# Hybrid decoder step on one core: output products of a batch moved between the sums of keys and of values, and the first batch of each layer prepared sooner

## What is computed

```python
kvc = _compress(concat([gather(pool_cmp), kv_c]), pe, w1, w2)      # chunk keys and values
# hid = silu(first half of chunk @ w1[:, :16] + second half @ w1[:, 16:]);  kvc = hid @ w2
blocks = _sel_blocks(concat([gather(pool_sel), kv_s]))             # pages by page_table
o_cmp, o_sel = _nsa_global(q_a, pos, kvc, blocks, slopes_a)        # chunk scores pick 16 blocks of 64 keys
o_win = _window_sample(q_a, win_all, n_win, slopes_a)              # last 512 keys
o_dil = _dilated_sample(q_b, dil_all, n_dil, slopes_b)             # strides 1, 4 and 16
y = _merge(o_cmp, o_sel, o_win, gate, o_dil, w_out)                # w_out for all rows together
```

## Time and profile before

| what | us |
|---|---|
| median of 3 runs | 2276.86 (2276.32 to 2280.13) |
| the profiled execution | 2278.07 |
| its span | 2276.2 |
| TensorE busy | 2142.7 (94%) |
| VectorE busy | 913.7 (40%) |
| POOL busy | 730.5 (32%) |
| ScalarE busy | 571.8 (25%) |
| batches of layer 0 | about 353 to 634 |
| batches of layer 1 | about 1471 to 1750 |

### The profile page before, as it was taken

How to read it: one execution, slowest core, us unless ns; L and a number is a source line. 1 busy time by engine, 2 the same in 40 slices (tenths; PEclk the granted TensorE clock), 3 DMA queues, 4 the chain that set the end, 5 groups by cost and what they waited for, 6 DMA issues and landing times.

```text
span 2276.2 us, 42319 instructions
## 1 busy us (share of the span) xinstructions
PE 2142.7 (94%) x12904; PEld 1516.7 (67%) x12904; DVE 913.7 (40%) x2434; ACT 571.8 (25%) x1404; POOL 730.5 (32%) x767
## 2 busy tenths in 40 slices
PE   7999997899899999999999999889989999999998
PEld 4545565676677777777745455657666677777776
DVE  2002763544553222336510147544455523233474
ACT  2101661212213322120111036421221232121202
POOL 0101772122243334434201037612224334343440
PEclk9999998999999999999999999999999999999999
DMA  9642026899964444554375320389999444444441
GB/s 349 235 166 84 19 57 195 279 282 290 287 221 167 172 172 181 195 196 172 119 277 203 131 72 0 91 266 276 293 295 301 172 166 179 173 172 172 180 165 42
DMA packets 130749, 424.92 MB, mean 187 GB/s; under 512 B 18337, under 2 KB 90274, under 8 KB 114082
## 3 DMA queue, kind: packets, MB, share of 16 engines
q1 hardware_dynamic: 108928, 326.01, 40.8%
q10 hardware_dynamic: 21666, 97.06, 14.2%
HBM read 412.40 MB, written 152.57 MB: 248 GB/s over the span
## 4 chain that ended last, share of the span: by engine, by line
PE 82%; DVE 6%; issue 4%; DMA 2%; SPq 2%; ACT 2%; POOL 1%; DVEq 0%; POOLq 0%; ACTq 0%
PE bank L1141 40%; PE bank L1224 14%; PE bank L1435 3%; PE bank L1443 3%; PE bank L1630 2%; PE bank L1404 2%; PE bank L1372 2%; PE bank L1384 2%; DVE zone L2113 2%; PE bank L1237 1%; PE bank L1455 1%; PE bank L1654 1%; POOL zone L975 1%; PE bank L1581 1%; DMA zone<-in_batch_rows 1%
## 5 line engine op out<-in xcount | busy, mean ns | idle before, releaser
L1141 PE MATMUL bank<-zone,ring 128*128 128x288 f32 x1664 | 424.8, 407 | 11.2 <-DVE zone L1793 8.5
L1141 PEld LDWEIGHTS bank<-zone,ring 128*128 128x128 f32 x1664 | 314.8, 190 | 104.2 <-DVE zone L1793 14.0
L1141 PE MATMUL bank<-zone,w 128*128 128x288 f32 x1408 | 353.5, 406 | 0.0
L1224 PE MATMUL bank<-ring,hT 128*128 128x512 f32 (+2 forms) x800 | 329.3, 565 | 6.5 <-ACTq L792 4.9
L1141 PEld LDWEIGHTS bank<-zone,w 128*128 128x128 f32 x1408 | 267.5, 190 | 73.9
L925 POOL TENSOR_TENSOR w<-ring 128x512 f32<-128x512 f32 x72 | 95.0, 1319 | 544.7 <-PE bank L1141 309.8
L1224 PEld LDWEIGHTS bank<-ring,hT 128*128 128x128 f32 (+1 forms) x800 | 147.2, 189 | 157.7 <-issue 151.8
L645 ACT COPY zone<-bank 128x288 f32<-128x288 f32 x72 | 28.7, 399 | 561.9 <-PE bank L1141 561.9
L1141 PE MATMUL bank<-xT,ring 128*128 128x288 f32 x512 | 137.3, 412 | 1.1 <-ACT zone L645 1.1
L1141 PEld LDWEIGHTS bank<-xT,ring 128*128 128x128 f32 x512 | 98.4, 193 | 29.5 <-ACT zone L645 2.0
L956 POOL COPY zone<-zone 128x128 f32<-128x128 f32 (+1 forms) x24 | 9.6, 399 | 327.8 <-ACT zone L710 327.8
(11 more groups left out here) (262 smaller groups left out, 3034.7 us busy)
## 6 DMA issues: line engine op xcount, KB each, us to landing
out_dil_s<-in_state_kv_dil SPq DMA_DIRECT2D x48, 2720.0 KB, 12.1
ring<-in_w_units SPq DMA_DIRECT2D x72, 1024.0 KB, 4.8
ring<-in_cache_kv_cmp SPq DMA_DIRECT2D x256, 128.0 KB, 4.9
ring<-in_cache_kv_sel SPq DMA_DIRECT2D x256, 128.0 KB, 9.0
zone<-in_batch_rows ACTq DMA_DIRECT2D x14, 2112.0 KB
zone<-in_batch_rows ACTq DMA_DIRECT2D x30, 768.0 KB, 6.6
ring<-in_w_in SPq DMA_DIRECT2D x10, 2048.0 KB, 8.0
zone<-in_batch_rows ACTq DMA_DIRECT2D x14, 1088.0 KB, 5.2
```

The source lines that it names most:

```text
L1141: last = mm(dst[:, 0:HALF], lhs[:, k, :], rhs(k), start=first and k == 0, stop=(k == 3), skip_group_check=True)
L1224: last = mm(dst, hT[:, k, t * P:t * P + ROWS[t]], ring[:, n % 2, k * CH:k * CH + width], start=start and k == 0, stop=stop and k == KT - 1)
```

## The change

Five edits, all in the order of work, none in the amount. On SP `page_numbers(1)` stands right behind the selected loads of batch 0. On POOL the strips are cleared and batch 0's queries copied as soon as the prompt's scores are biased; add_pairs and new_keys follow, and only the padding waits for `og_d`. On TensorE the chunk output product goes in front of the window output, and `first_of_odd(1)` and `both_of_sum(it + 1, 0)` go in front of the output products. On VectorE the copy of the output products goes into the next `hidden_batch`, between the first `inverse` and the second `even_sums`.

```diff
@@ sync
                 load_selected(page)
+                page = page_numbers(1)
                 for s in range(STG):
...
                 load_window(sp, l, 0)
-                page = page_numbers(1)
@@ gpsimd
-                add_pairs(l * NB)
-                pool.wait_ge(og_d.sem, og_d.at(l, ROUNDS))
-                pool.sem_inc(waits_taken_pool, 1)
...
                 def new_keys(it, b):
-                    pool.wait_ge(s_pad.sem, s_pad.at(it, 1))
                     pool.wait_ge(kda_ld.sem, kda_ld.at(it, 1))
...
+                pool.wait_ge(a_sb.sem, a_sb.at(l, 2 * STEPS_L))
+                pool.sem_inc(waits_taken_pool, 1)
                 nc.gpsimd.memset(strips.rearrange("p a x -> p (a x)"), 0.0).then_inc(s_clear.sem, 1)
                 pool.wait_ge(s_clear.sem, s_clear.at(l, 1))
                 pool.sem_inc(waits_taken_pool, 1)
                 batch_queries(0)
+                add_pairs(l * NB)
+                new_keys(l * NB, 0)
+                pool.wait_ge(kd_new.sem, kd_new.at(l * NB, 1))
+                pool.wait_ge(og_d.sem, og_d.at(l, ROUNDS))
+                pool.sem_inc(waits_taken_pool, 1)
                 pad(l * NB)
-                new_keys(l * NB, 0)
@@ tensor, batch
                     pe.wait_ge(sc_used.sem, sc_used.at(it, 0))
+                    pe.wait_ge(kv_act.sem, kv_act.at(it, 2))
+                    pe.sem_inc(waits_taken_pe, 1)
+                    O = bank[6][:, 0:P]
+                    mm(O[low], ptc, vc, start=True, stop=True, skip_group_check=True)
                     pe.wait_ge(ptk_act.sem, ptk_act.at(it, 2))
                     pe.sem_inc(waits_taken_pe, 1)
-                    O = bank[6][:, 0:P]
                     for c in range(4):
                         mm(O[high], ptw[:, c, :], kw_sb[:, c, 128:256], start=(c == 0), stop=False, skip_group_check=True)
-                    mm(O[high], ptw[0:64, 4, :], vsm[:, 128:256], start=False, stop=True, skip_group_check=True)
-                    pe.wait_ge(kv_act.sem, kv_act.at(it, 2))
-                    pe.sem_inc(waits_taken_pe, 1)
-                    mm(O[low], ptc, vc, start=True, stop=True, skip_group_check=True).then_inc(win_pv.sem, 1)
+                    mm(O[high], ptw[0:64, 4, :], vsm[:, 128:256], start=False, stop=True, skip_group_check=True).then_inc(
+                        win_pv.sem, 1)
...
                         first_of_odd(0, HID_BANK)
+                    if more:
+                        first_of_odd(1, HID_BANK)
+                        both_of_sum(it + 1, 0, HID_BANK)
                     B = bank[SC_BANK[SC_OUT]]
...
                     if more:
-                        first_of_odd(1, HID_BANK)
-                        both_of_sum(it + 1, 0, HID_BANK)
                         both_of_sum(it + 1, 1, HID_BANK)
@@ vector
+                def keep_outputs(b):
+                    it = l * NB + b
+                    dve.wait_ge(sc_full.sem, sc_full.at(it, SC_OUT + 1))
+                    dve.sem_inc(waits_taken_dve, 1)
+                    V.tensor_copy(hT[:, :, ds(b * NS + SEQ, NS)],
+                                  bank[SC_BANK[SC_OUT]][:, 0:64].rearrange("p (q t) -> p q t", q=8)).then_inc(sc_used.sem, 1)
+                    dve.wait_ge(sc_used.sem, sc_used.at(it, U_OUT + 1))
+                    dve.sem_inc(out_put.sem, 1)
...
                     inverse(0)
+                    if between is not None:
+                        between()
                     even_sums(1, added)
...
-                    B = small(SC_OUT)
-                    V.tensor_copy(hT[:, :, put], B[:, 0:64].rearrange("p (q t) -> p q t", q=8)).then_inc(sc_used.sem, 1)
-                    dve.wait_ge(sc_used.sem, sc_used.at(it, U_OUT + 1))
-                    dve.sem_inc(out_put.sem, 1)
...
                     batch(b)
-                    hidden_batch(l * NB + b + 1, HID_BANK)
+                    hidden_batch(l * NB + b + 1, HID_BANK, lambda: keep_outputs(b))
                 batch(NB - 1)
+                keep_outputs(NB - 1)
```

More of the change, by code:

```diff
@@ L2086, in _, with hidden_batch @@
                 prompt_steps(l, ROUNDS - 1, AHEAD, STEPS + AHEAD, True)
-                def hidden_batch(it, at):
+                def keep_outputs(b):
[6 more added lines that the diff above has]
+                    dve.sem_inc(out_put.sem, 1)
+                def hidden_batch(it, at, between=None):
                     horder = Order(ch_h, it)
@@ L2139, in batch @@
                     order = Order(ch_s, it)
-                    new, put = ds(b * 64, 64), ds(b * NS + SEQ, NS)
+                    new = ds(b * 64, 64)
                     def new_scores(dst, src, bias, least):
```

## The result

The changed kernel takes 2242.58 us (median of four runs, 2241.82 to 2249.43) against 2276.59 for the one before, beside which it ran: a ratio of 0.9858 with a 95% interval of 0.9832 to 0.9885. The forecast was 2241.5. The profiled execution took 2241.82 us; on its page TensorE is as busy in absolute terms and busier as a share (before: 2142.7 us, 94%), and only the span shrank.

A forecast was written before the change was run, and what follows sets the result against it. TensorE works almost all the time, so only its waits, lower clock and in-line work can give time back. 21.9 + 5.8 + 10.5 - 2.8 = 35.4 us off, forecast 2241.5 us, range 2231 to 2257.

The forecast's parts named there:

- The stall: Batch 0, both layers: TensorE no longer waits for raw pages; 13.1 us in layer 0, 8.8 in layer 1, together 21.9.
- it moves 9.4 us of SP's register loads: SP, batch 0: page-number reads go behind the selected loads, costed at nothing, up to 9.4 us without that cover.
- Even with the worst landing of before, 11.5 us: Raw-page loads of batch 1: out by 364.3, in at 375.8 at worst; expected under 4 us, about 368.
- What is late next is nothing of the loads: After the raw-page wait in batch 0 goes, the next thing late is the ordinary chain, not a load.
- The start of batch 0: Queries and new keys sooner: first products at 353.5, 4 us sooner; first step on chunk scores at 360.5, net 2.1 us.
- Chunk values first: TensorE, each batch: two chunk-value products move into 0.65 us of idle time; 16 x 0.36 = 5.8 us.
- Outputs between the sums: Passage between batches: first sums 1.26 us sooner, 0.5 paid on VectorE, net 0.75 (0.45 to 1.03); 14 passages give 10.5 us.
- What DMA takes back: Steady periods: the same loads in a shorter period cost 0.2 us per passage, 14 x 0.2 = 2.8 us.
- The DMA rival: DMA binds steady periods, which stay at 34.3 us; 21.9 and some 1 us are left: 2255. Chance 0.2.
- the forecast's own sign of being wrong: TensorE waiting for selected pages or late keys over 0.5 us each batch, or VectorE waiting for output products.
- The clock rival: Later periods of both layers: three clock drops go too, 3 x 1.5 = 4.6 us more, 2237. Chance 0.25.

## Why the prediction was right, and where it was not

- **The stall** was the largest term, 21.9 us with the sooner start. The first periods and the starts won 11.1 + 8.5 and 1.9 + 2.8 us, together 24.3; 1.4 of it belong to the steady edits (two passages) and 1.6 to a further drop of the clock that only the kernel before has in layer 1's first period, which leaves 21.3. The mechanism is shown: with the page numbers read late, the wait comes back at 19.6 and 17.8 us.
- What was not seen: I took the 8.1 and 5.1 us for fixed. They hang on how soon behind the raw pages the dilated values are issued, and the sooner queries bring the two together. The step "it moves 9.4 us of SP's register loads" was right and the price too low for what it guards: beside the sooner queries it is worth 39 us. The sum came out right since both edits are in the change; the reason given, pages issued in front of the key and value loads, is what the runs bear out.
- "Even with the worst landing of before, 11.5 us": 20.3 us has been seen since. The conclusion held because the raw pages now meet no large load; the last of them landed after 3.4 us at 368.1 (forecast "under 4 us, about 368"), the slowest after 4.6.
- "What is late next is nothing of the loads" holds for the profiled execution (0.6 us of selected pages at most) but not in general: in three other kernels with early page numbers it is 2.2 to 3.1 us.
- **The start of batch 0**: TensorE starts it at 353.75 (forecast 353.5), L2165 comes at 361.08 instead of 360.5, 1.5 us sooner and not 2.1. Most of the 0.6 lies ahead of the reciprocal, which starts at 355.31 and not 354.9: the prompt's last products start 0.9 us later than before (352.73 against 351.85) where 0.6 was allowed, and TensorE was 0.45 us behind before any pair sum was wanted. From the reciprocal on it took 5.77 us and not 5.6, with the clock low from 358 to 361. The later steps gave back 0.36 as said: L1645 is 1.9 sooner.
- **Chunk values first**: the idle time before L1607 is 0.29 us (forecast 0.3). Alone the part gave 0.3 a period.
- **Outputs between the sums**: 1.33 us won (1.26), 0.62 paid (0.5), net 0.72 (0.75, bounds 0.45 to 1.03). The reading of the Trainium skill, "VectorE: DVE Perf Modes", section "The DRAIN you can't avoid", by which the exchange would be 0.23, is not borne out: there are 0.28 and 0.34 us of waiting on either side of the copy, and moving copy and wait brought 0.4 a period.
- **What DMA takes back** was the term most off: 0.2 us a passage forecast, 0.55 found (0.77 ahead of the late keys' products, 0.22 behind them). The periods should have come to 33.3; they are 33.7. Without it (late keys moved) they are 33.20, the forecast's figure for a period that DMA doesn't disturb.
- **The DMA rival** was half right: not the selected pages but the late keys bind, and they bound half of the gain, not the whole of it. By the forecast's own sign of being wrong, more than 0.5 us a batch at the late L1524, this came close: the twelve waits there are 0.3 to 1.0 us, eight of them over 0.5.
- **The clock rival**: the periods of both layers hold one drop instead of three (apart from the stall's), so two thirds of it came true, some 3 us. The unexpected side is that there are seven in each kernel without the late keys' wait.
- That the total was met within 1.1 us owes something to chance. The twelve later periods won 10.1 us against 10.9 forecast, and 1.6 of that is a drop of the clock that didn't come; layer 1's first period was spared another; and the stretch behind the last batch, which apart from its chunk product (0.4) the change doesn't touch, was 1.8 us shorter. Without these three the time would have been some 5 us longer, still well inside the range.

## What to carry to other kernels

A wait on a load at the edge of a loop is not a constant: before pricing an edit near it, look at what else is issued in the same few microseconds, since a sooner start can make it longer, and have the loads that are waited for issued well ahead of the large ones. Parts of a change that share such a wait need not add up; take one part back out of the whole as well as trying it alone. When a short wait of TensorE goes, count the clock's drops before and after; work that fills the waits left may be worth more than the wait that went.

## What the runs showed of the hardware

- Three 128 KB pages issued up to 2.1 us ahead of a 2112 KB load of the other queue landed 17.6 to 20.3 us after their issue (8.0 at most with that load issued 16 us behind the last page), and for the last 2 us the core's DMA was nearly idle (share 0.10 and 0.04): an earlier issue by 1 to 2 us did not bring a small load in ahead of a large one. In the changed kernel and the one with the page numbers alone, where the large load came 9.8 us or more behind the last page, there was no wait.
- Late keys landed in a median of 5.6 us when issued on SP's queue ahead of sixteen raw pages, and in 6.9 on ScalarE's queue with the first pages 1.7 us ahead, at the same point of the period; with no raw pages beside them in 6.4 and 5.4.
- Seven drops of the granted clock to 0.50 in fourteen periods, 1.6 us each, behind waits of 0.42 and 1.00 us on VectorE; 0.59 and 0.63 us of repeated products in these waits took six of them away. Nearly the same waits, 0.34 and 1.00 us, had one drop in fourteen periods in the changed kernel.
- VectorE's small step L2111 took 1.26 us with POOL's clearing of the strips beside it, and 0.30 (L2125) with the clearing moved away.
